# Paged decode attention on one core: key pages loaded in four groups of heads and block-transposed on VectorE

## What is computed

```
k_past = cache_k[page_table].reshape(8, 2048, 16, 64)      # 8.4 MB for each sequence
v_past = cache_v[page_table].reshape(8, 2048, 16, 64)      # 8.4 MB for each sequence
s_past = einsum('nqhd,nkhd->nhqk', q, k_past) * 64**-0.5 + cq - c_past     # 4 query rows x 16 heads
p = softmax(concat([s_past, s_new]), -1)
out = einsum('nhqk,nkhd->nqhd', p_past, v_past) + einsum('nhqk,nkhd->nqhd', p_new, v_new)
```

## Time and profile before

| | us |
|---|---|
| median of 3 runs (1629.01 to 1629.26) | 1629.07 |
| the profiled execution's own time | 1625.25 |
| its span (first to last instruction) | 1623.5 |
| one turn of the attention loop, 858.7 to 920.6 | 61.9 |
| PE / DVE / ACT busy in that turn | 59.3 / 32.9 / 23.2 |

### The profile page before, as it was taken

How to read it: one execution, slowest core, us unless ns; L and a number is a source line. 1 busy time by engine, 2 the same in 40 slices (tenths; PEclk the granted TensorE clock), 3 DMA queues, 4 the chain that set the end, 5 groups by cost and what they waited for, 6 DMA issues and landing times.

```text
span 1623.5 us, 37862 instructions
## 1 busy us (share of the span) xinstructions
PE 1455.5 (90%) x15152; PEld 1040.5 (64%) x15152; DVE 471.8 (29%) x1112; ACT 328.7 (20%) x696; POOL 118.5 (7%) x176
## 2 busy tenths in 40 slices
PE   4988999999399999589999999999999599999991
PEld 4877988888244444356555656655545488888881
DVE  3330010000122332365545555555413301000103
ACT  2120110111111111333333434433211011110110
POOL 1012000000200000101001000000000210000002
PEclk9789999999799999799999999999998699999995
DMA  8256999999931131677988987987753069999975
GB/s 245 125 217 205 390 393 390 377 381 395 327 135 41 38 102 38 210 249 258 317 280 275 314 294 269 316 280 277 296 233 136 20 215 397 388 386 397 394 280 182
DMA packets 121996, 424.59 MB, mean 262 GB/s; under 512 B 26519, under 2 KB 40920, under 8 KB 113471
## 3 DMA queue, kind: packets, MB, share of 16 engines
q1 hardware_dynamic: 90439, 367.60, 61.8%
q0 software_dynamic: 10448, 29.73, 6.1%
q10 hardware_dynamic: 21040, 26.29, 4.7%
HBM read 393.70 MB, written 30.24 MB: 261 GB/s over the span
## 4 chain that ended last, share of the span: by engine, by line
PE 59%; DMA 16%; issue 14%; DVE 4%; ACT 3%; SPq 3%; POOL 1%; ACTq 1%; DVEq 0%; POOLq 0%
DMA W<-in_w_up 14%; PE PS L969 10%; PE PS L856 6%; PE PS L1110 6%; PE PS L852 6%; PE PS L887 4%; PE PS L882 4%; PE PS L1176 3%; PE PS L1128 3%; PE PS L1094 3%; PE PS L791 3%; PE PS L1055 2%; PE PS L1075 1%; DMA KB<-yd,SLi 1%; SPq L396 1%
## 5 line engine op out<-in xcount | busy, mean ns | idle before, releaser
L852 PE MATMUL PS<-W,VB 128*32 128x384 f32 x3072 | 353.2, 492 | 15.7 <-DMA W<-in_w_up 6.7
L856 PE MATMUL PS<-W,VB 128*32 128x128 f32 x3072 | 352.0, 275 | 5.5 <-issue 5.4
L856 PEld LDWEIGHTS PS<-W,VB 128*32 128x32 f32 x3072 | 335.3, 111 | 11.6 <-issue 9.6
L882 PE MATMUL PS<-W,VB 128*32 128x384 f32 x1536 | 174.7, 492 | 5.6 <-ACT VB L1326 5.6
L1110 PE MATMUL PS<-C,KB 128*128 128x128 f32 x1024 | 168.5, 296 | 9.4 <-ACT W L1491 7.7
L887 PE MATMUL PS<-W,VB 128*32 128x128 f32 (+1 forms) x1024 | 174.7, 329 | 0.0
L1110 PEld LDWEIGHTS PS<-C,KB 128*128 128x128 f32 x1024 | 118.4, 148 | 74.8 <-issue 59.8
L1755 DVE TENSOR_TENSOR VB<-VB,PS 128x384 f32<-128x384 f32 x32 | 17.7, 554 | 511.4 <-PE PS L868 470.5
L852 PEld LDWEIGHTS PS<-W,VB 128*32 128x32 f32 x3072 | 144.5, 110 | 28.8 <-DMA W<-in_w_up 12.2
L887 PEld LDWEIGHTS PS<-W,VB 128*32 128x32 f32 x1024 | 102.2, 110 | 16.0 <-issue 0.2
L1491 ACT ACTIVATE W<-PS 128x512 f32<-128x512 f32 x128 | 76.1, 595 | 169.4 <-PE PS L1110 164.2
(11 more groups left out here) (261 smaller groups left out, 1589.9 us busy)
## 6 DMA issues: line engine op xcount, KB each, us to landing
W<-in_w_gate SPq DMA_DIRECT2D x32, 2048.0 KB
W<-in_w_up SPq DMA_DIRECT2D x32, 2048.0 KB, 21.6
W<-in_w_down SPq DMA_DIRECT2D x32, 2048.0 KB, 11.3
KB<-in_cache_k SPq DMA_DIRECT2D x128, 512.0 KB, 5.2
W<-in_cache_v SPq DMA_DIRECT2D x64, 512.0 KB, 5.5
VB<-in_cache_v SPq DMA_DIRECT2D x64, 512.0 KB, 7.3
yd<-VB ACTq DMA_DIRECT2D x32, 288.0 KB, 7.0
W<-in_w_kvf SPq DMA_DIRECT2D x4, 2048.0 KB, 15.7
```

Source lines behind the costliest of these rows:

```text
L852: pe.matmul(PS[32 * q:32 * q + 32, bank, 0:WIDE], x, w[:, k, 0:WIDE], start=(k == 0), stop=(k == KC - 1), tile_position=(0, 32 * q), skip_ ...
L856: mm = pe.matmul(PS[CAP:P, bank, P * q:P * q + P], x, w[:, k, WIDE:FF], start=(k == 0 and q == 0), stop=(k == KC - 1), tile_position=(0, C ...
L882: pe.matmul(PS[32 * q:32 * q + 32, 5 + n, 0:WIDE], h, w[:, f, n * WIDE:n * WIDE + WIDE], start=(f == 0), stop=(f == FC - 1), tile_position ...
```

## The change

Keys are no longer transposed on TensorE. Each page is loaded in four DMAs, one for each group a of four heads: 256 columns of all 128 rows go to partitions 32a to 32a+31, as 4 pieces of 256 floats for each partition. VectorE then transposes each page in place in blocks of 32x32 (`keys_transposed`, in even ticks). After that a partition holds one of 32 dimensions for 128 rows, so that a score matmul takes a strided view of KB directly, with 512 columns: 8 matmuls per chunk instead of 16, and no PSUM evacuation and no KTR. A contraction over 128 rows holds two half heads for each of four groups. QBLK, the bias rows, the new keys, the values and the output transposes follow the new order of heads; `out_transposes` does 4 blocks instead of 2. `pts` moves from DVE to ACT. Value pages move from SP's to ACT's queue, one chunk behind each `values` step, and `values` runs a chunk at a time instead of a page. The new rows' keys and queries are transposed by VectorE once (KQR, KQ4) ahead of the loop, and the last tile's keys and queries now share the scratch tile TS. `s_ready` of the last chunk is waited for ahead of the first output projection.

```diff
-QK_TICK = [2 * x + 3 for x in range(KTICKS // 2)]
+TICKS = V_TICK[-1] + 1
+K_TICK = [2 * g for g in range(PAGES)]
+QK_TICK = (7, 15, 23, 31)
+SCORE_TICK = (8, 16, 24, 32)
...
-O_TICK = [g + 8 for g in range(PAGES + 1)]
-OT_TICK = 27
+O_TICK = (7, 15, 23, 29)
+OB_TICK = 30
+OT_TICK = 32
...
+        def load_chunk(eng, dst, rows, i, ch, s, keys=False):
+            pages = nc.values_load_multi_w_load_instructions(
...
+                if keys:
+                    for a in range(4):
+                        eng.dma_start(to[32 * a:32 * a + 32, :].rearrange("p (c f) -> p c f", c=4),
+                                     src[:, 256 * a:256 * a + 256].rearrange("(c t) f -> t c f", t=32)).then_inc(s, 16)
+                else:
+                    eng.dma_start(to, src).then_inc(s, 16)
...
-                    sp.wait_ge(sem("kt_tr"), 32 * i + 8 * (ch + 1))
+                    sp.wait_ge(sem("qk_done"), 4 * i + ch + 1)
...
-                    if not (isinstance(i, int) and i == 0 and ch < 2):
-                        load_chunk(VSL[ch], v_rows, i, ch, sem(f"v_in{ch}"))
+                    if isinstance(i, int) and i == 0 and ch >= 2:
+                        load_chunk(sp, VSL[ch], v_rows, i, ch, sem(f"v_in{ch}"))
...
+                def qk(ch):
+
+                    pe.wait_ge(sem("kt_done"), 16 * i + CH * ch + CH)
...
+                    for e in range(2):
+                        for a in range(4):
+                            b = 2 * a + e
+                            mm = pe.matmul(PS[32 * a:32 * a + 32, ch % 2, :], QBLK[:, b, :], ks[:, :, 32 * b:32 * b + 32],
+                                           start=(e == 0), stop=(e == 1), tile_position=(0, 32 * a), skip_group_check=True)
+                    mm.then_inc(sem("qk_done"), 1)
...
-                dst = TS if t < 4 else QT4
-                if t < 4:
-                    act.wait_ge(sem("ktd_out"), 32 * (t + 1))
+                dst = TS
+                act.wait_ge(sem("ktd_out"), 32 * (t + 1))
...
+                        if front and n - 1 in O_TICK:
+
+                            ch = O_TICK.index(n - 1)
+                            act.wait_ge(sem("pv_done"), NCH * i - NCH + ch + 1)
+                            settled(act)
+                            load_chunk(act, VSL[ch], v_rows, i, ch, sem(f"v_in{ch}"))
...
+                def keys_transposed(g):
+
+                    ch = g // CH
+                    if g % CH == 0:
+                        dve.wait_ge(sem(f"k_in{ch % 2}"), 256 * (2 * i + ch // 2 + 1))
+                    page = KB[:, ch % 2, g % CH * D:g % CH * D + D]
+                    dve.transpose(page, page).then_inc(sem("kt_done"), 1)
```

More of the change, by code:

```diff
@@ L491, in _ @@
                     .then_inc(sem(f"proj_in_{'kvq'[which // 2]}"), 16)
[L493 to L497, removed]
             def load_bias(i, half):
                 for a in range(4):
-                    src = RPD[4 * a:4 * a + 4, 8 * half + PAGES * i:8 * half + PAGES * i + 8, :] if isinstance(i, int) else \
-                        RPD[4 * a:4 * a + 4, bass.ds(PAGES * i + 8 * half, 8), :]
+                    src = RPD[a:NH:4, 8 * half + PAGES * i:8 * half + PAGES * i + 8, :] if isinstance(i, int) else \
+                        RPD[a:NH:4, bass.ds(PAGES * i + 8 * half, 8), :]
                     src = src.rearrange("h (o g) r -> h o (g r)", o=1).to_broadcast([4, NS, D])
@@ L1114, in qk @@
[L1114 to L1119, removed]
-                        pe.wait_ge(sem("qb_ready"), i + 1)
[L1121 to L1130, removed]
+                def qk(ch):
+                    pe.wait_ge(sem("kt_done"), 16 * i + CH * ch + CH)
+                    if ch == 0:
+                        pe.wait_ge(sem("qb_ready"), i + 1)
+                    after(pe, sem("s_ready"), 4 * i + ch - 1)
+                    settled(pe)
+                    ks = KB[:, ch % 2, :].rearrange("p (x n) -> p x n", n=256)
+                    for e in range(2):
[3 more added lines that the diff above has]
+                                           start=(e == 0), stop=(e == 1), tile_position=(0, 32 * a), skip_group_check=True)
@@ L1159, in p_transposes, with values @@
                     mm.then_inc(sem("ptt_tr"), 1)
-                def values(g):
-                    ch = g // CH
-                    if g == 0:
+                def values(ch):
+                    if ch == 0:
                         after(pe, sem("ots_ready"), 2 * i - 2)
[L1167 to L1177, removed]
-                    if g == PAGES:
-                        mm.then_inc(sem("o_mm"), 1)
-                    elif g % CH == CH - 1:
-                        mm.then_inc(sem("pv_done"), 1)
@@ new lines, in values @@
+                    pe.wait_ge(sem("ptt_ready"), 5 * i - 5 + ch + 1)
+                    pe.wait_ge(sem(f"v_in{ch}"), 64 * i)
+                    for g in range(CH):
+                        for a in range(4):
+                            v = paged(VSL[ch])[:, g, :].rearrange("p (x a d) -> p a x d", a=4, d=DH)[:, a]
+                            mm = pe.matmul(PS[32 * a:32 * a + 32, 5, 0:256], PTT[:, CH * ch + g, 32 * a:32 * a + 32], v,
+                                           start=(ch == 0 and g == 0), stop=False, tile_position=(0, 32 * a), skip_group_check=True)
@@ L1183, in attention, with out_transposes @@
+                def out_transposes():
+                    pe.wait_ge(sem("ob_ready"), i)
+                    pe.wait_ge(sem("sn_ready"), i + 1 if front else i)
+                    settled(pe)
+                    for a in range(4):
+                        at = (P - NS) * a
+                        mm = pe.transpose(PS[:, 2 if front else 7, at:at + P], OB[:, a].rearrange("p u d -> p (u d)"), ident)
+                    mm.then_inc(sem("ob_tr"), 1)
                 for n in range(TICKS + shift):
@@ L1184, in attention @@
                     m = n - shift
+                    if back and n in O_TICK:
+                        values(O_TICK.index(n))
                     if front:
-                        if n < KTICKS:
-                            k_tick(n)
                         if n in QK_TICK:
```

198 lines of the change are left out of this document (98 added, 100 removed).

## The result

The changed kernel took 1734.63 us (median of 4 runs, 1728.96 to 1738.07) where the kernel before took 1629.04 on the same chip: a ratio of 1.065, with a 95% interval of 1.061 to 1.070. The forecast was 1614, its range 1578 to 1668, and "faster" was held likelier than "slower". The direction and the size were wrong. The place was right: the attention turns decide, and the landing of keys is part of what they wait for.

A forecast was written before the change was run, and what follows sets the result against it. TensorE's queue was taken to bound the attention turn, then transfers: seven turns from 61.9 to 59 us (-20.3), +4.7 +1 -1, is -15.6 on 1625.25, or 1609.7; with 3.8 for the median, 1614, range 1578 to 1668.

The forecast's parts named there:

- the transfers' sum of 59.6 us a turn: Attention turn: keys 35.3 us plus other transfers 24.3; taken as 59 us, deciding the turn instead of the engines' chain.
- all else (9.5 MB at 391) 24.3: Attention turn's transfers other than keys: 9.5 MB at MoE 0's 391 GB/s, 24.3 us a turn.
- The second rival: Attention turn: key loads held to the stores' 200 GB/s, 42 + 24.3 = 66.3 us a turn, 1664 us; chance 0.27.
- the chain of 53.4 us: Engines in an attention turn: ten prompt units 34.8 us, plus key transposes, score blocks, maxima and the turn's border.
- The first rival: Attention turn: transfers hardly suffer and hide, the engines' chain decides, turn 55.5 us, time 1588 us; chance 0.25.
- DVE's transpose: Key pages in the attention turn: sixteen VectorE transposes of 128x1024, taken at 1.2 us each.
- the third rival: Attention turn: VectorE transposes cost twice as much, 2.4 us each, turn 65.4 us, time 1658 us; chance 0.12.
- DVE busy 36.5 a turn: VectorE in the attention turn: from 32.9 us, copies go and sixteen transposes come, giving 36.5 us busy.
- PE "stops being the bound": TensorE in the attention turn: 14.3 us of key transposes go, it needs under 46 us and no longer bounds.
- ACT at some 30: ScalarE in the attention turn: 9.5 us of copies go, 4.6 and 16 value DMAs come; some 30 us.
- SP's queue: Attention turn: key DMAs at 0.58 us each, 47.3 us a turn with bias DMAs; hidden, below 61.9.
- the wait for the keys' landing: Ahead of the attention loop: the last tile's queries wait until its keys land in DRAM, 4.7 us later.

The follow-up runs named there:

- e1_full_rows: The changed kernel with each key page loaded by one DMA of 128 partitions and 4-KB rows instead of four of 32 partitions: 1671.87 us, ratio 1.024.
- e12: The changed kernel with each key page in two DMAs of whole rows into partitions 0 to 63 and 64 to 127: 1743.91 us, ratio 1.068.
- e14: The changed kernel with the value pages of turns 1 to 7 on SyncE's queue, key DMAs in ascending order: 1735.37 us, ratio 1.076.
- e10: The changed kernel with a page's key DMAs in the order 0, 2, 1, 3 and value pages on SyncE's queue: 1728.95 us, ratio 1.060.
- e7: The changed kernel with full-row key DMAs and each VectorE transpose cut from 1024 to 32 columns: 1636.86 us, ratio 1.006.
- e13: The changed kernel, narrow key DMAs kept, with its VectorE transposes cut to 32 columns: 1702.18 us, ratio 1.053.
- e2: The changed kernel with four key DMAs a page, each filling 256 columns of all 128 partitions from 32 page rows: 2089.15 us, ratio 1.279.

## Why the prediction was wrong

**The step that failed is the transfers' sum of 59.6 us a turn**, the first of two. It was 35.3 us for keys and "all else (9.5 MB at 391) 24.3"; the turn measured 73.5 us, with the DMA engines busy throughout. Three terms make up the 13.9 us between them:

- Keys: 8192 packets a turn at 75 ns over 16 engines are 38.4 us, 3.1 more than taken. That is 219 GB/s, where 238 was taken and 200 was the bound, so this term was nearly right.
- Values: 2048 packets at 232 ns are 29.7 us, where 8.4 MB at 391 GB/s are 21.5. Of these 8.2 us, 5.6 are the rise from 188 to 232 ns beside the narrow key loads, for which the sum had no term. The other 2.6 were there before the change: at the 188 ns of the attention turns then, the same packets are 24.1 us and not the 21.5 of MoE 0's rate.
- The rest (bias, prompt loads, small packets) is 5.4 us where 2.8 was taken.

The prediction had the better base in its own words: a DMA share of 0.86, "that is 53.2 us" a turn, where the rate of MoE 0 gives 45.8. With the 14.3 us that keys rose (24.1 to 38.4) and the 5.6 of the values it comes to 73.1. Even with keys at the forecast's own 35.3, and nothing for the values, it would have been 64.4, above the 61.9 of before. The second rival had the right mechanism, and its 66.3 is 7 too small: its 42 for keys (and the 44 estimated beside it) was more than the 38.4 that were measured, and its 24.3 for all else was 11 too little.

**The second step that failed is the chain of 53.4 us.** It was held to be under the transfers, so its error was hidden. e1_full_rows, where transfers don't bind, has a turn of 65.5. The sum left out the four blocks of value matmuls, which the chain of waits shows in it (L1161, 15.9% of 65 us, 10.3), and ScalarE's DMA issues (3.6), which I had put under busy time beside other work; 53.4 + 10.3 + 3.6 = 67.3. It also priced PE's part at full clock. Even with wide transfers the change would have lost 39 us. The first rival, "transfers hardly suffer", 1588, was thus no real case: with its condition met as nearly as a run here does it, by full-row keys, the time is 1672.

**The other steps.** DVE's transpose: 1.2 us taken, 1.237 measured; the third rival is out. DVE busy 36.5 a turn: 36.9. PE "stops being the bound": right, at 49 to 55 us busy instead of under 46, for the clock that I didn't see coming. ACT at some 30: 18.4 busy, and some 8 of issues (16 at 0.5). SP's queue: a key DMA blocks 0.317 us with 0.50 from one to the next where 0.58 was taken, but with the engines full single ones block up to 3.97. Hidden it was not: it is 22.5% of the chain in the turn above, though e12, with half as many key DMAs and a turn of 75.6, shows that their number is not the cause. Ahead of the loop, the wait for the keys' landing:

```profile
666.76 1.30 ACTq L1470 DMA_DIRECT2D ktd<-VB  x2
671.82 0.69 ACT L1409 ACTIVATE VB<-PS,qg 128x512 f32<-128x512 f32 x1 [5.08 <-DMA ktd<-VB]
```

4.7 was forecast; 5.1 us is the wait and 4.5 the delay of the first scores. This term isn't firm, though: the first scores of kernels with the same code up to there start between 679.6 (e14) and 691.6 (e10), each profiled once. The first turn was put at -1 and is +12.1, since sixteen transposes (19.8 us of DVE) came into a turn that before was as short as 50.8; e7 and e13, at 51.1 and 51.3, show that it is they. The end was +1 and is +7.4, of which 3.3 lie in the projections up to the last tile's; what the other 4.1 are wasn't tried.

Of the signs named in advance, "a turn over 62 with DVE idle until key landings, and a share near 1 at under 280 GB/s" came in full.

## What to carry to other kernels

Before splitting a load by partitions, ask which partitions each DMA writes at one time and what else uses the engines. Here DMAs into 32 or 64 adjacent partitions had slow packets of their own and slowed those of the wide DMAs on another queue, while the share of the DMA engines rose to 1 and looked like demand. Price the rest of the transfers at the rate of the stage itself, not at that of another stage. If a load must be narrow, try DMAs that follow each other going to different halves (2.1% here). And when the bound engine is relieved, sum the chain that takes over with every block that stands in it (the DMA issues of a compute engine too) and expect TensorE at a lower clock once it waits.

## What the runs showed of the hardware

- 4-KB packets took 169 to 188 ns in mean where every load went to all partitions or to every second one on 16 engines (201 in e2, whose key loads moved at 96 GB/s). Where keys went into 32 or 64 adjacent ones they took 227 to 270 with values on a queue of their own, and 190 to 197 with all on SyncE's. 1-KB packets took 69 to 76 ns into 32 partitions; into all partitions they took 47, with two to three tenths of the engines busy.
- Key DMAs in the order 0, 2, 1, 3 of the partition groups instead of 0, 1, 2, 3: 75 to 70 ns a packet, 2.1% of the time.
- A DMA whose source's outermost dimension has 4 steps moved 96 GB/s with two tenths of the engines busy.
- Ten matmuls a turn that compute nothing raised the granted TensorE clock from 0.81 to 0.94 and cost no time.
- VectorE's transpose of 128x1024 4-byte values in blocks of 32x32 takes 1.237 us in place.
